# Modulation tiles taken in units of four, and the first down projection with operands and weights split in two parts

## The reference, cut to what matters

```python
mod = (s_lat @ w_ada[l] + b_ada[l]).reshape(B, N_MOD, 1, D)
mod_c = (s_ctx @ w_ada[l] + b_ada[l]).reshape(N_MOD, 1, 1, D)
...
def conv_ffn(h, w_up, conv_w, conv_b, w_down):
    g, u = jnp.split(h @ w_up, 2, axis=-1)
    g = dwconv(g, conv_w) + conv_b
    return (jax.nn.silu(g) * u) @ w_down
...
        x_lat = x_lat + g2 * conv_ffn(rmsnorm(x_lat, norm_ffn[layer]) * (1 + sc2) + sh2, *ffn_p[layer])
```

## Time and profile before

| | |
|---|---|
| median of three runs | 4245.91 us (4243.02 to 4247.62) |
| the profiled execution | 4245.91 us |
| its span on the core | 4244.0 us |
| mean granted TensorE clock | 0.917 of full |
| TensorE matmuls busy | 3545.1 us (84%) |
| VectorE, ScalarE busy | 1671.6 us (39%), 865.2 us (20%) |
| first down projection, first matmul to last evacuation | 3145.8 to 3375.7 us |
| modulation tiles in the four products | 677.5 to 3122.0 us, 128 of them |

### The profile page before, as it was taken

How to read it: one execution, slowest core, us unless ns; L and a number is a source line. 1 busy time by engine, 2 the same in 40 slices (tenths; PEclk the granted TensorE clock), 3 DMA queues, 4 the chain that set the end, 5 groups by cost and what they waited for, 6 DMA issues and landing times. The chain is left out here.

```text
span 4244.0 us, 68832 instructions
## 1 busy us (share of the span) xinstructions
PE 3545.1 (84%) x29998; PEld 2774.8 (65%) x29998; DVE 1671.6 (39%) x2987; ACT 865.2 (20%) x1444; POOL 56.9 (1%) x74
## 2 busy tenths in 40 slices
PE   5879988588987577774989976899989978979997
PEld 3768986556747233333746846888878865577887
DVE  3645544562133100004545256444420154245644
ACT  2135430042101011112011151211100112323321
POOL 0000000000000100000000000000000000000000
PEclk7979998799987799997999988999999989989998
DMA  6130005203331799994521100244431010013322
GB/s 222 52 125 4 4 12 188 85 11 108 111 115 60 307 424 422 424 422 144 157 88 55 51 2 30 76 113 121 117 95 55 1 48 25 1 35 98 91 80 80
DMA packets 379411, 494.21 MB, mean 116 GB/s; under 512 B 15994, under 2 KB 325787, under 8 KB 370436
## 3 DMA queue, kind: packets, MB, share of 16 engines
q1 hardware_dynamic: 369588, 456.12, 31.1%
q0 software_dynamic: 4432, 25.70, 1.6%
q10 hardware_dynamic: 5120, 8.39, 0.5%
HBM read 458.70 MB, written 31.47 MB: 115 GB/s over the span
## 5 line engine op out<-in xcount | busy, mean ns | idle before, releaser
L302 PE MATMUL banks<-leading,w_rest 128*128 128x512 f32 (+2 forms) x1920 | 698.7, 364 | 58.8 <-DVE w_rest L262 58.8
L302 PE MATMUL banks<-rest,w_leading 128*128 128x512 f32 (+2 forms) x1920 | 691.2, 360 | 0.0
L302 PE MATMUL banks<-leading,w_leading 128*128 128x512 f32 (+2 forms) x1920 | 691.0, 360 | 0.0
L302 PEld LDWEIGHTS banks<-leading,w_rest 128*128 128x128 f32 (+1 forms) x1920 | 365.0, 190 | 119.0 <-DVE w_rest L262 46.4
L302 PE MATMUL banks<-w_rest,leading 128*128 128x256 f32 (+3 forms) x1332 | 394.6, 296 | 55.5 <-DVE w_rest L262 55.5
L262 DVE TENSOR_TENSOR w_rest<-land,w_leading 128x1024 fp32r<-128x1024 f32 (+3 forms) x296 | 280.0, 988 | 356.6 <-ACT w_leading L256 356.6
L302 PEld LDWEIGHTS banks<-leading,w_leading 128*128 128x128 f32 (+1 forms) x1920 | 364.5, 190 | 59.2
L302 PEld LDWEIGHTS banks<-rest,w_leading 128*128 128x128 f32 (+1 forms) x1920 | 364.9, 190 | 57.5
L256 ACT CAST w_leading<-land 128x1024 fp32r<-128x1024 f32 (+3 forms) x296 | 239.4, 856 | 743.9 <-DMA land<-in_w_in 283.8
L302 PE MATMUL banks<-w_leading,rest 128*128 128x256 f32 (+3 forms) x1332 | 390.5, 293 | 0.0
L302 PE MATMUL banks<-w_leading,leading 128*128 128x256 f32 (+3 forms) x1332 | 390.0, 293 | 0.0
(11 more groups left out here) (537 smaller groups left out, 4721.7 us busy)
## 6 DMA issues: line engine op xcount, KB each, us to landing
wg<-in_w_exp_gate SPq DMA_DIRECT2D x32, 2048.0 KB, 28.4
wu<-in_w_exp_up SPq DMA_DIRECT2D x32, 2048.0 KB, 28.4
wd<-in_w_exp_down SPq DMA_DIRECT2D x32, 2048.0 KB, 27.9
ws<-in_ada_w SPq DMA_DIRECT2D x96, 512.0 KB, 3.9
land<-in_w_in SPq DMA_DIRECT2D x41, 1024.0 KB, 5.5
land<-in_ffn_up SPq DMA_DIRECT2D x44, 512.0 KB, 5.4
land<-in_ffn_up SPq DMA_DIRECT2D x88, 256.0 KB, 3.3
ws<-in_w_ada SPq DMA_DIRECT2D x32, 512.0 KB, 3.9
```

Source lines behind the costliest of these rows:

```text
L302: mm = nc.tensor.matmul(bank_of(r, kind, at), lhsT, rhs, start=(k == 0 and q == 0), stop=(k == kt - 1 and q == len(each) - 1))
```

## The change

`modulation_tiles` gives units of four tiles (512 columns). A unit is loaded and multiplied in four pieces, each of two blocks of the contraction (256 rows x 512 columns). In a piece the four quarters of the result hold the four tiles, and no longer four partial sums of one tile; each accumulates over all eight blocks. The copy is made once a unit, at its last piece; the turn once a unit, after the second piece of the next, with eight columns (two of each quarter, picked out of the identity); the addition once a unit, at the third piece of the next.

The first down projection becomes a split product with eight banks and four chunks. Its weights enter the list of those brought ahead. Its operand `fT` is split inside the product (`whole`): ScalarE rounds the blocks of a chunk and VectorE subtracts, before the weights of the same step, in the steps of the first job alone. The remainder is written in the place of `fT` itself, the rounded part in a new buffer. In `normed`, the buffer `whole` has one slot instead of four where the result is not split.

```diff
@@ -93,6 +93,7 @@
+PIECES = 4
@@ -147,6 +148,7 @@
+            (a["ffn_down_0"][:, 0:256], 0, -(-KF // 4), 256),
@@ -190,13 +192,14 @@
-        side_w = [ctx.enter_context(nc.sbuf_tensor(f"ws_{nc.next_id()}", [P, KD, P], F32)) for _ in range(SIDE_SLOTS if side else 0)]
+        side_w = [ctx.enter_context(nc.sbuf_tensor(f"ws_{nc.next_id()}", [P, KD // PIECES, 512], F32)) for _ in range(SIDE_SLOTS if side else 0)]
...
+            pair_columns = m.ident.rearrange("p (g c) -> p g c", g=4)[:, :, 0:2]
@@ -212,12 +215,14 @@
             def sides_between(r0, r1):
...
-                return range(-(-r0 * len(side) // total), -(-r1 * len(side) // total))
+                n = PIECES * len(side)
+                return range(-(-r0 * n // total), -(-r1 * n // total))
...
             def _(sp):
                 def load_side(t):
-                    sp.dma_start(side_w[t % SIDE_SLOTS][:, :, :], side[t][0].rearrange("(k p) n -> p k n", p=P)
+                    k0 = KD // PIECES * (t % PIECES)
+                    sp.dma_start(side_w[t % SIDE_SLOTS][:, :, :], side[t // PIECES][0][k0 * P:(k0 + KD // PIECES) * P, :].rearrange("(k p) n -> p k n", p=P)
@@ -235,19 +240,34 @@
-                        for t in range(min(SIDE_SLOTS, len(side))):
+                        for t in range(min(SIDE_SLOTS, PIECES * len(side))):
...
-                            if t + SIDE_SLOTS < len(side):
+                            if t + SIDE_SLOTS < PIECES * len(side):
...
+            def round_operands(act, s):
...
+                x, hi, lo = whole
+                for k in range(steps[s][4], steps[s][5]):
+                    nc.scalar.copy(hi[:, k, :], x[:, k, :]).then_inc(own_rounded_sem, 1)
...
+            def part_operands(dve, s):
...
+                x, hi, lo = whole
+                for k in range(steps[s][4], steps[s][5]):
+                    dve.wait_ge(own_rounded_sem, k + 1)
+                    nc.vector.tensor_tensor(lo[:, k, :], x[:, k, :], hi[:, k, :].bitcast(F32), ALU.subtract).then_inc(own_parted_sem, 1)
...
             def round_weights(act, s):
+                if whole is not None and steps[s][0] == 0:
+                    round_operands(act, s)
@@ -256,6 +276,8 @@
             def part_weights(dve, s):
+                if whole is not None and steps[s][0] == 0:
+                    part_operands(dve, s)
@@ -264,10 +286,24 @@
             def bank_of(r, kind, at):
...
-            def side_turn(pe, t):
...
-                pe.wait_ge(side_copied_sem, t + 1)
-                nc.tensor.matmul(m.ps[:, 6 + t % 2, P:P + 2], side_rows[t % 2][:, :], m.pick2[:, 0:2], start=True, stop=True).then_inc(side_turned_sem, 1)
+            def side_turn(pe, u):
...
+                pe.wait_ge(side_copied_sem, u + 1)
+                nc.tensor.matmul(m.ps[:, 6 + u % 2, P:P + 8], side_rows[u % 2][:, :], pair_columns, start=True, stop=True).then_inc(side_turned_sem, 1)
...
+            def side_piece(pe, t):
...
+                u, k0 = t // PIECES, KD // PIECES * (t % PIECES)
+                pe.wait_ge(side_landed_sem[t % SIDE_SLOTS], 16 * (t // SIDE_SLOTS + 1))
+                if k0 == 0 and u >= 2:
+                    pe.wait_ge(side_read_sem, u - 1)
+                for k in range(k0, k0 + KD // PIECES):
+                    for g in range(4):
+                        mm = nc.tensor.matmul(m.ps[32 * g:32 * (g + 1), 6 + u % 2, 0:P], m.cond_wide[:, k, :],
+                                              side_w[t % SIDE_SLOTS][:, k - k0, g * P:(g + 1) * P], start=(k == 0), stop=(k == KD - 1))
+                mm.then_inc(side_made_sem, 1)
+                if t % PIECES == 1 and u:
+                    side_turn(pe, u - 1)
@@ -297,31 +333,25 @@
+                            if whole is not None and i == 0 and j == 0:
+                                pe.wait_ge(own_parted_sem, k + 1)
...
-                                pe.wait_ge(side_landed_sem[t % SIDE_SLOTS], 16 * (t // SIDE_SLOTS + 1))
-                                if t >= 2:
-                                    pe.wait_ge(side_read_sem, t - 1)
-                                for k in range(KD):
-                                    g = k % 4
-                                    mm = nc.tensor.matmul(m.ps[32 * g:32 * (g + 1), 6 + t % 2, 0:P], m.cond_wide[:, k, :], side_w[t % SIDE_SLOTS][:, k, :],
-                                                          start=(k < 4), stop=(k >= 4))
-                                mm.then_inc(side_made_sem, 1)
-                                if t:
-                                    side_turn(pe, t - 1)
+                                side_piece(pe, t)
...
-            def side_add(dve, t):
...
-                dve.wait_ge(side_turned_sem, t + 1)
-                nc.vector.tensor_scalar(side[t][2], m.ps[:, 6 + t % 2, P:P + 2], side[t][3], None, ALU.add).then_inc(side_read_sem, 1)
+            def side_add(dve, u):
...
+                dve.wait_ge(side_turned_sem, u + 1)
+                turned = m.ps[:, 6 + u % 2, P:P + 8].rearrange("p (f j) -> p f j", j=2)
+                nc.vector.tensor_tensor(side[u][2], turned, bc(side[u][3].unsqueeze(2), 2), ALU.add).then_inc(side_read_sem, 1)
@@ -344,10 +374,12 @@
             def read_both(dve, r, count, j, kind, at):
...
-                    dve.wait_ge(side_made_sem, t + 1)
-                    nc.vector.tensor_copy(side_rows[t % 2][:, :], m.ps[:, 6 + t % 2, 0:P]).then_inc(side_copied_sem, 1)
-                    if t:
-                        side_add(dve, t - 1)
+                    u = t // PIECES
+                    if t % PIECES == PIECES - 1:
+                        dve.wait_ge(side_made_sem, t + 1)
+                        nc.vector.tensor_copy(side_rows[u % 2][:, :], m.ps[:, 6 + u % 2, 0:P]).then_inc(side_copied_sem, 1)
+                    elif t % PIECES == 2 and u:
+                        side_add(dve, u - 1)
@@ -406,7 +438,7 @@
-    return [(w[:, f * P:(f + 1) * P], m.cond[:, i, :, :], m.mod[:, i, f, :], bias[:, f:f + 1]) for f in range(first, end)]
+    return [(w[:, f * P:(f + 4) * P], m.cond[:, i, :, :], m.mod[:, i, f:f + 4, :], bias[:, f:f + 4]) for f in range(first, end, 4)]
@@ -444,7 +476,7 @@
-        b.sq, b.diag, b.whole, b.ss, b.root, b.rstd, b.gain = buffers(nc, ctx, sq=[2, D], diag=[n, P], whole=[4, 512], ss=[n], root=[n], rstd=[n], gain=[len(kinds), KD])
+        b.sq, b.diag, b.whole, b.ss, b.root, b.rstd, b.gain = buffers(nc, ctx, sq=[2, D], diag=[n, P], whole=[4 if parts else 1, 512], ss=[n], root=[n], rstd=[n], gain=[len(kinds), KD])
@@ -1775,7 +1807,7 @@
-        products(nc, m, jobs, xT, evac, "vector", kt=kt, wslots=wslots, width=width, split=split, banks=banks, k_chunks=k_chunks)
+        products(nc, m, jobs, xT, evac, "vector", kt=kt, wslots=wslots, width=width, split=split, banks=banks, k_chunks=k_chunks, whole=whole)
@@ -2168,7 +2200,11 @@
-                m.fT = two_parts(nc, c1, KF, LAT) if layer else buffers(nc, c1, fT=[KF, TOK])[0]
+                if layer:
+                    m.fT = two_parts(nc, c1, KF, LAT)
+                else:
+                    up = c1.enter_context(ExitStack())
+                    (m.fT,) = buffers(nc, up, fT=[KF, TOK])
@@ -2180,7 +2216,11 @@
-                    project_add(nc, m, a["ffn_down_0"], lambda k, t0, tn, j: m.fT[:, k, t0:t0 + tn], KF, adds(c1, 5), width=256, wslots=2)
+                    up.close()
+                    rest = c1.enter_context(nc.sbuf_tensor("first_up_rest", [P, KF, TOK], F32R))
+                    tiles = adds(c1, 5)
+                    leading = c1.enter_context(nc.sbuf_tensor("first_up_leading", [P, KF, TOK], F32R))
+                    project_add(nc, m, a["ffn_down_0"], of_halves((leading, rest)), KF, tiles, width=256, split=True, banks=8, k_chunks=4, whole=(m.fT, leading, rest))
```

8 lines of the change are left out of this document (4 added, 4 removed).

## The result

| | before | after |
| --- | --- | --- |
| median of 4 runs of each, same chip | 4244.65 us (4243.02 to 4247.62) | 4176.63 us (4176.16 to 4177.4) |
| profiled execution: time, span | 4245.91, 4244.0 us | 4177.06, 4175.2 us |
| granted clock over the span | 0.917 | 0.917 |

The kernel is faster: ratio 0.9839, with a 95% interval of 0.9822 to 0.9856, so 68.0 us between the medians, where 69.7 was predicted.

The account below looks back on a forecast made before the run. TensorE, busy 84% of the span, was taken as the bound. The projection's 37.8 + 2.8 + 0.3 = 40.9 us and the modulation's 23.0 + 5.8 = 28.8 give 69.7: 4245.9 to 4176.2 us, range 4163 to 4198.

Parts of the forecast that it names:

- The price of a turn: Modulation products: each turn removed frees 0.24 us of TensorE's stream, 23.0 us for 96 turns.
- The lower bound: Modulation turns: only the turn's weights count, 188 ns each, 18.0 us in all.
- the upper: Modulation turns: the second main matmul's extra 0.08 us goes too, 0.32 us a turn, 30.7 us in all.
- The rival with empty slots: Modulation products: main matmuls wait for the array to drain anyway, so turns save nothing; 4199.2 us, chance 0.05.
- I take all 5.8 us: Hyena product: all seven TensorE waits for VectorE's late addition vanish, 5.8 us; bounds 0 and 5.8.
- What is late next there is nothing on the rows: Hyena product: once the addition waits go, no other TensorE wait is expected; the only other one is the start.
- the 22 added waits: Down projection: TensorE's waits for own operands, bounded by nothing and 0.1 us each, taken as nothing, 2 us left in range.
- The operand rival: Down projection's first job: TensorE waits for every operand chunk's rest, 14.6 us come back; 4190.8 us, chance 0.05.
- the weight-load rival: Down projection: 1584 weight loads of 0.19 us stand open before their matmuls; some 4477 us, chance 0.01.
- The rival on the other side: Down projection: one landing slot serialises it, up to 7.5 us at 15 step boundaries; 4288.7 us, chance 0.02.
- Landing plus 1.7 us exceeds the step of 13.0: Down projection: threshold where the single landing slot decides, a landing of 11.3 us, against 5.8 seen.
- first result takes longer: Down projection: first result exceeds later ones by 2.0 us before, 1.7 in the second down projection; 0.3 less.

Follow-up runs that it names:

- late_turns: The kernel before, in the hyena product alone with four banks and four row buffers, each turn two tiles behind instead of one: 4237.06 us.
- late_3: The kernel after with three small loads (128x256), each waited for, before every weight load of the first down projection, on the same queue: 4209.58 us.
- four_banks: The kernel before with its modulation tiles spread over four PSUM banks, so matmuls wait for the addition four tiles back instead of two: 4247.18 us.
- weights_first: The kernel after with the first down projection's first weights rounded and parted ahead of the first operand chunks: 4176.07 us.
- both_further: The kernel after with branch projections also split, and first-step weights ahead of operands there and in the first down projection: 4160.16 us, ratio 0.9792.

## Why the prediction was right

| step | predicted | measured |
| --- | --- | --- |
| attention, 24 turns | 5.8 | 6.0 |
| branches, 12 turns | 2.9 | 3.0 |
| hyena, 24 turns and the waits | 5.8 + 5.8 | 12.9 |
| up, 36 turns | 8.6 | 8.1 |
| down projection | 40.9 | 40.75 |
| the rest | 0 | -1.9 |
| sum (span) | 69.7 | 68.8 |

The price of a turn, 0.24 us, was read from starts. Putting turns back gives 0.22, 2 us less over 96; taking them out of the three stages without such waits gave (6.0 + 3.0 + 8.1) / 72 = 0.24. The lower bound (188 ns, 18.0 us) and the upper (0.32) are both too far out; the upper assumed that the second matmul's delay goes with the turn, and it grows by 0.02 instead. The rival with empty slots did not occur.

The hyena waits were mis-sized, and in two ways. The step "I take all 5.8 us" took the whole of the waits: in after 2.4 us of waits are left (2.0 for side loads, 0.4 for a copy), so "What is late next there is nothing on the rows" fell too. And the prediction has no term for the clock, while late_turns against before shows 3.6 us of matmuls at half clock behind the two longest waits. Both together are worth 7.6 us in after where 5.8 were taken. This and the turn's price nearly cancel: 5.3 + 7.6 = 12.9, against 11.6. So the mechanism holds in that VectorE's lateness was the loss, and its size came out by errors on both sides. That the sum lies within 2 us of the measured gain is luck in part as well, for the stages that nothing touched vary by more than that.

The down projection came out by its own steps. The evacuations that open jobs 1 and 4 in after, and the stage's last:

```profile
3157.31 0.42 DVE L1807 TENSOR_TENSOR t<-banks,gate_rows 128x256 f32<-128x256 f32 x1 [12.45 <-PE banks L340]
...
3299.87 0.42 DVE L1807 TENSOR_TENSOR t<-banks,gate_rows 128x256 f32<-128x256 f32 x1 [12.45 <-PE banks L340]
...
3307.07 0.42 DVE L1807 TENSOR_TENSOR t<-banks,gate_rows 128x256 f32<-128x256 f32 x1 [0.55 <-PE banks L340]
```

(3299.87 - 3157.31) / 3 = 47.52 us a job, which is 7.92 us for each of its 6 results and 0.1200 for each of its 396 matmuls: the figure that the earlier trace rows gave. The formula of the Trainium skill ("TensorE: Matmul & The Clock Gate", Back-to-back issue gap) that stood beside it (109.2 ns) would have made a result 7.21 us, and the trace disagrees here as in the earlier trace rows. The section gives it for isolated matmuls and says itself that in a stream of weight loads and matmuls both set the spacing, which the prediction left out. From TensorE's start to the last evacuation it is 192.26 us, and 229.93 before: 37.7 saved, where 37.8 + 0.3 was predicted. The start came after 7.37 us in place of 7.6, since a chunk took VectorE 5.30 / 6 = 0.88 us and not 0.915; that saves 3.1 and not 2.8.

TensorE's waits in the down stage, 3080 to 3320 us, show what did not happen:

```profile
PE banks L340 <- DVE w_rest L284: 8.6, 1, 8.6
```

The only other waits in that window are at matmuls before and behind the projection. Within it there is one wait, at the start. None at a step boundary, none for an own operand, as predicted; so the 22 added waits cost nothing that can be seen. The operand rival would have shown here, and the weight-load rival in the job spacing. By the rule of the Trainium skill behind that one ("TensorE: Matmul & The Clock Gate", What overlaps and what doesn't) the loads would stand open; with 0.194 us for a load and 0.120 for a matmul they do not.

The rival on the other side was rightly put aside, but its threshold was wrong. "Landing plus 1.7 us exceeds the step of 13.0" frees the slot when half the block is parted. late_3 shows 2.7 us, for both halves, and the four steps of a job share their slack, so the mean step of 11.9 counts: a landing of 9.2 us, not 11.3. The expectation for late_3 had the 2.6 and the 11.9 right already, but it took over the prediction's landing of 5.8 us, which is that of the first load in the earlier trace rows. A load lands after 4.3 us in the median here, so that late_3 comes to 11.4 and not 13.3 us, and 15 x 1.9 = 28 us were expected too much.

## What to carry to other kernels

Where TensorE is full in a stage, price an instruction in its stream by the difference of two periods with and without it, and price the work of the other engines at nothing until a row shows TensorE waiting for it. Take the pace of a new form from a product of the same form elsewhere in the same kernel: it came out to four digits here. And a wait of TensorE can cost more than it lasts: look at the granted clock behind it, and when the wait is taken away, compare TensorE's busy time for the same matmuls as well as its idle time. Look also for what it waits for next.

## What the hardware showed that was not expected

A wait of 1.9 us within the hyena product of before was followed, twice, by 3.4 us at half clock, while behind waits of 0.4 us there and of 1.0 to 1.2 us in four_banks and late_turns the granted clock stayed at 1.00. The rows do not say what else it takes. The matmuls just before and behind all of these waits are tiles or turns of the modulation.

After its wait of 8.6 us TensorE began the down projection at half clock. The stretches 3114.80 to 3118.80 and 3119.40 to 3125.00 us of after (columns as in the earlier trace rows):

```profile
3114.80:3118.80 4.00, 3.99 (x18) 3.99 (x19) 4.00 (x5) 3.28 (x5) 0.00 (x0) 0.50 0.48 157
3119.40:3125.00 5.60, 5.60 (x49) 5.60 (x48) 5.60 (x7) 5.07 (x7) 0.00 (x0) 1.00 0.20 57
```

At the granted 0.50 (1.2 GHz) it issues 18 matmuls in 4.0 us, 0.22 us each; at 1.00 (2.4 GHz) the pace is 0.12. Eighteen at 0.10 us more are 1.8 us, and this explains the "first result takes longer" that the prediction had read as 1.7 without a cause; in the second down projection of before the granted clock is 0.59 over the first 4 us. It also shows where the rest of the 3.4 us of weights_first went. The first evacuation of job 1 follows TensorE's start by 43.08 us there and by 42.50 in after. The first groups of three matmuls start about 0.85 us apart, near VectorE's 0.88 us a chunk, where three at half clock take 0.66.

A split matmul of 512 columns takes 0.23 us from start to start in the branch product of both_further, against 0.120 for 256 columns; an fp32 one is two records, 0.2158 us each for 256 columns. So three split matmuls cost 0.36 us where one fp32 matmul costs 0.43, and the weight load of 0.19 us lies inside both.

```profile
1176.04 0.39 PE L358 MATMUL banks<-branch_leading,w_rest 128*128 128x512 f32 x1
1176.27 0.39 PE L358 MATMUL banks<-branch_rest,w_leading 128*128 128x512 f32 x1
1176.49 0.39 PE L358 MATMUL banks<-branch_leading,w_leading 128*128 128x512 f32 x1
```
